# Matmul operands at multiples of 512 bytes, and 512-column products issued as two groups of 256 columns

## The reference

```python
# first block, one layer
h = h + _hybrid_mixer(_rmsnorm(h, ...), ..., w_in, ..., w_out)   # retention, gated delta, gated linear
h = h + _memory_cross_attn(_rmsnorm(h, ...), mem_n, wq, wk, wv, wo)
h = h + _conv_ffn(_rmsnorm(h, ...), ffn_up, ffn_conv_w, ffn_down)
# second block, two layers
for l in range(2):
    z = rms_norm(x, g_attn[l]) @ w_in[l]
    ...                                # MLA, dilated and top-k attention on slices of z
    x = x + mix @ w_o[l]
    u = causal_dwconv(rms_norm(x, g_ffn[l]) @ w_up[l], conv_w[l], conv_b[l])
    gate, up = u[..., :D_FF], u[..., D_FF:]
    x = x + (jax.nn.silu(gate) * up) @ w_down[l]      # D_FF = 2816
return rms_norm(x, g_final)
```

## The kernel before

| operand | slot 0 | slot 1 |
|---|---|---|
| `w_hi` | 384 | 0 |
| `w_lo` | 128 | 256 |
| `hT_hi`, `hT_lo` | 192 | 192 |
| `a_hi`, `a_lo` | 480 | 480 |

## Time and profile before

### The profile page before, as it was taken

The page is one execution under the profiler, slowest core; times in us unless marked ns, Lnnn a source line. Parts: engine busy times, 40 slices in busy tenths (PEclk is TensorE's granted clock), DMA queues, the critical chain, the costliest instruction groups (busy, mean ns, idle before and its releaser), DMA issues.

```text
span 1482.9 us, 20646 instructions
## 1 busy us (share of the span) xinstructions
PE 1306.5 (88%) x7800; PEld 1161.0 (78%) x7800; DVE 886.5 (60%) x1502; ACT 637.9 (43%) x1007; POOL 41.7 (3%) x51
## 2 busy tenths in 40 slices
PE   6993885679888899998898988999979899799996
PEld 6982664568778789997896667999979766699995
DVE  5436665542664676766656547676664664766674
ACT  4443101112544455554544345555544433555553
POOL 0000211000200000000000000000000000000000
PEclk9995766887999999999897589999999957899998
DMA  8430000001442455453430034454345101454541
GB/s 329 172 129 28 0 0 29 1 1 57 142 151 105 153 191 202 179 196 120 178 142 29 1 130 158 177 205 173 138 171 193 57 1 56 161 196 173 204 174 42
DMA packets 20228, 183.26 MB, mean 124 GB/s; under 512 B 2368, under 2 KB 2640, under 8 KB 4560
## 3 DMA queue, kind: packets, MB, share of 16 engines
q1 hardware_dynamic: 19040, 178.09, 33.2%
q0 software_dynamic: 1136, 4.46, 0.9%
HBM read 181.49 MB, written 1.05 MB: 123 GB/s over the span
## 4 chain that ended last, share of the span: by engine, by line
PE 80%; DVE 11%; ACT 5%; issue 1%; POOL 1%; DMA 1%; SPq 0%; DVEq 0%; ACTq 0%; POOLq 0%
PE ps L486 21%; PE ps L488 21%; PE ps L487 21%; PE ps L656 3%; PE ps L637 3%; PE ps L647 2%; PE ps L772 2%; PE ps L745 1%; ACT z L1026 1%; ACT hT_hi L1036 1%; DVE arena L1823 1%; ACT w_hi L1016 1%; DVE arena L1605 1%; DVE w_lo L1329 1%; PE ps L954 1%
## 5 line engine op out<-in xcount | busy, mean ns | idle before, releaser
L1329 DVE TENSOR_TENSOR w_lo<-raw,w_hi 128x2048 fp32r<-128x2048 f32 (+4 forms) x252 | 390.8, 1557 | 167.7 <-ACT w_hi L1016 167.1
L1016 ACT ACTIVATE w_hi<-raw 128x2048 fp32r<-128x2048 f32 (+4 forms) x252 | 332.2, 1325 | 215.4 <-PE ps L488 200.9
L486 PE MATMUL ps<-hT_hi,w_hi 128*128 128x256 f32 x1184 | 336.8, 284 | 8.2 <-DVE hT_lo L1378 8.2
L488 PE MATMUL ps<-hT_hi,w_lo 128*128 128x256 f32 x1184 | 335.0, 283 | 0.0
L487 PE MATMUL ps<-hT_lo,w_hi 128*128 128x256 f32 x1184 | 334.8, 283 | 0.0
L486 PEld LDWEIGHTS ps<-hT_hi,w_hi 128*128 128x128 f32 x1184 | 228.9, 193 | 13.7 <-issue 7.8
L487 PEld LDWEIGHTS ps<-hT_lo,w_hi 128*128 128x128 f32 x1184 | 228.4, 193 | 2.8
L488 PEld LDWEIGHTS ps<-hT_hi,w_lo 128*128 128x128 f32 x1184 | 228.6, 193 | 0.0
L486 PE MATMUL ps<-w_hi,hT_hi 128*128 128x378 f32 (+2 forms) x576 | 209.7, 364 | 18.2 <-DVE hT_lo L1463 9.6
L487 PE MATMUL ps<-w_lo,hT_hi 128*128 128x378 f32 (+2 forms) x576 | 207.8, 361 | 0.0
L488 PE MATMUL ps<-w_hi,hT_lo 128*128 128x378 f32 (+2 forms) x576 | 207.7, 361 | 0.0
(11 more groups left out here) (274 smaller groups left out, 1462.3 us busy)
## 6 DMA issues: line engine op xcount, KB each, us to landing
raw<-in_ffn_b SPq DMA_DIRECT2D x63, 1536.0 KB, 6.4
raw<-in_win SPq DMA_DIRECT2D x16, 1512.0 KB, 6.4
raw<-in_win SPq DMA_DIRECT2D x10, 1552.0 KB, 6.5
raw<-in_wo SPq DMA_DIRECT2D x12, 1024.0 KB, 4.8
raw<-in_wk SPq DMA_DIRECT2D x4, 1024.0 KB, 4.7
raw<-in_wv SPq DMA_DIRECT2D x4, 1024.0 KB, 4.8
raw<-in_wout SPq DMA_DIRECT2D x4, 1024.0 KB, 4.8
raw<-in_wq SPq DMA_DIRECT2D x4, 1024.0 KB, 4.7
```

The lines of the kernel that those rows point to most:

```text
L486: pe.matmul(out, a_hi_, b_hi, start=start, stop=False)
L488: return pe.matmul(out, a_lo_, b_hi, start=False, stop=stop)
L1016: act.activation(w_hi[:, slot, a:b], raw[:, slot, a:b], ACT.Copy).then_inc(hi_done, 1)
L1329: dve.tensor_tensor(w_lo[:, slot, a:b], raw[:, slot, a:b], w_hi[:, slot, a:b].bitcast(F32), ALU.subtract).then_inc(lo_done, 1)
```

## The change

1. The operands of the matmuls (`a_hi`, `a_lo`, `hT_hi`, `hT_lo`, `w_hi`, `w_lo`) and then `raw` are declared first, behind a filler `lead` of 96 elements, and a slot grows from 3104 to 3200 elements (12,800 bytes, 25 times 512). The scratch for POOL's transfers shrinks from 16,384 to 8,192 bytes, which makes the room. In the built program `a_hi` is now at 8,704, `a_lo` at 10,752, `hT_hi` at 12,800, `hT_lo` at 20,992, `w_hi` at 29,184, `w_lo` at 54,784: all of them, and both slots, at multiples of 512. The moving weights of the column stages still start at many remainders, since their rows stay 1,552 and 1,512 bytes long.
2. In the row stages a new helper `mm3_halves` makes two groups of three matmuls over 256 columns each out of every group of three over 512. `start` is set for the first half alone and `stop` for the second alone.

```diff
-SLOT = 3104
+SLOT = 3200
+LEAD = 96
...
-        raw = sb("raw", [P, 2, SLOT])
+        sb("lead", [P, LEAD])
+        a_hi = sb("a_hi", [P, 2, T], F32R)
+        a_lo = sb("a_lo", [P, 2, T], F32R)
+        hT_hi = sb("hT_hi", [P, KT, T], F32R)
+        hT_lo = sb("hT_lo", [P, KT, T], F32R)
         w_hi = sb("w_hi", [P, 2, SLOT], F32R)
         w_lo = sb("w_lo", [P, 2, SLOT], F32R)
+        raw = sb("raw", [P, 2, SLOT])
...
-        hT_hi = sb("hT_hi", [P, KT, T], F32R)
-        hT_lo = sb("hT_lo", [P, KT, T], F32R)
...
-        a_hi = sb("a_hi", [P, 2, T], F32R)
-        a_lo = sb("a_lo", [P, 2, T], F32R)
...
+            def mm3_halves(bank, a_hi_, a_lo_, b_hi, b_lo, start, stop):
+
+                for c in (slice(0, 256), slice(256, 512)):
+                    ins = mm3(bank[:, c], a_hi_, a_lo_, b_hi[:, c], b_lo[:, c], start and c.start == 0, stop and c.start > 0)
+                return ins
...
-                                ins = mm3(ps[:, 2 * t + half, :], hT_hi[:, k, t * P:(t + 1) * P],
+                                ins = mm3_halves(ps[:, 2 * t + half, :], hT_hi[:, k, t * P:(t + 1) * P],
...
-                            ins = mm3(ps[:, 2 * t + half, :], a_hi[:, a, t * P:(t + 1) * P],
+                            ins = mm3_halves(ps[:, 2 * t + half, :], a_hi[:, a, t * P:(t + 1) * P],
...
-                        ins = mm3(ps[:, 2 * t + half, :], a_hi[:, 1, t * P:(t + 1) * P], a_lo[:, 1, t * P:(t + 1) * P],
+                        ins = mm3_halves(ps[:, 2 * t + half, :], a_hi[:, 1, t * P:(t + 1) * P], a_lo[:, 1, t * P:(t + 1) * P],
...
-    nc = bacc.Bacc("TRN2", target_bir_lowering=False, num_devices=1)
+    nc = bacc.Bacc("TRN2", target_bir_lowering=False, num_devices=1, dynamic_dma_scratch_size=8192)
```

## The result

The changed kernel takes 1498.84 us in the median of 4 runs (1497.09 to 1499.74), the kernel before 1481.84 us in the median of 4 runs beside them. The ratio is 1.016 (95% interval 1.009 to 1.023). On another chip, with 6 and 17 runs, it was 1.011 (1.009 to 1.014). So the change costs 1.1 to 1.6%, 17 us between the medians, where I had forecast 33 to 37 us less.

What follows compares the result with a forecast made beforehand. TensorE's mm3 matmul pace was taken as the bound; (19.2 + 10.8 + 5.1 + 2.6) x 0.96 = 36.2 us off the profiled span 1482.9 gave 1446.7, forecast as a 1449 us median, 2.5% faster, range 1430 to 1474.

Steps and rivals of the forecast that it cites:

- What bounds the kernel: Feed-forward: TensorE is busy throughout, so the pace of mm3's matmuls decides the time and only a shorter pace shortens it.
- The reading of the two slots: up and stage V: slots differ only in address, and both operands' sides matter, by about 4 ns a matmul.
- I take 113.5 - 3.3 = 110.2 ns: Aligned 256-column matmuls: slot 1's pace less stage V's moving-operand effect, assuming the two effects add.
- my upper bound of 113.5: Aligned 256-column matmuls: slot 1's pace in ns, if the moving operand's 192 costs nothing; lower bound 109.4.
- Transposed stages: 3,552 matmuls going from 115.6 to 110.2 ns, 19.2 us less.
- Row stages: Split 512-column products at 220.4 ns a pair: down 10.8 us less, square stages 5.1 us less.
- Column stages: Stationary side aligned, moving side mixed: 2.1 ns less for each of 1,248 matmuls, 2.6 us.
- Share at the full clock: Whole kernel: about 3% of matmuls run at the lower clock, so the summed gain is multiplied by 0.96.
- no effect of addresses: Rival: slots differ by something accompanying them, such as DVE and ACT work; 1484 or 1489 us, chance 0.09.
- partial: Rival: effects do not add, 113.5 ns is the fp32r floor at 256 columns; 1471 us, within 2%, chance 0.28.
- My slower rival: Row stages: the second load of the same operand is exposed, a pair takes 380 ns; 1643 us, chance 0.03.
- if they still differ, the address was not it: Check in up: both slots should take about 5.29 us for 48; slots still differing would rule out the address.

Runs made afterwards that it cites:

- the faster layouts: Changed kernel with whole 512-column products, hT at 192, w at 0 (mod 256), a_hi and a_lo at 192 or 160: ratios 0.988 and 0.991 (192), 0.988 (160).
- `a` at 480: Changed kernel with whole 512-column products, hT at 192, w at 0, a_hi and a_lo at 480 (224 mod 256): 1481.73 us, ratio 0.999.
- Kernels of TensorE alone: Whole computation left out, only runs of fp32r matmuls with weight loads at varied operand starts and orders; 256 columns at difference 0 took 120.0 ns.
- one layout: Changed kernel with whole 512-column products, hT at 192, w at 0, a_hi and a_lo at 160 (mod 256): 1467.99 us, ratio 0.988.
- the feed-forward that stayed at 117.8 behind difference 192: Changed kernel, whole 512-column products, hT and a at 192, w at 0 (mod 256), one feed-forward per profile at 8.42 us rounds: ratio 0.988, again 0.991.
- hT at 64: Changed kernel with whole 512-column products, hT_hi and hT_lo at 64, w and a at 0 (mod 256): 1483.67 us, ratio 1.003.

## Why the prediction was wrong

- *What bounds the kernel*: right. The pace of `mm3`'s matmuls decided, no wait ahead of them grew by more than 0.1 us, and the smaller scratch cost nothing that shows (it is in all the faster layouts too, though no run changes it alone).
- *The reading of the two slots*: the step that failed. I took "the stationary operand goes to 0 and 256, 4.2 ns less" and "in stage V the moving operand makes that step, 3.3 ns less" for two effects, one of each operand's own remainder. The runs show a pace that goes with the difference of the two starts instead: it went from 192 to 64 in `up` and from 64 to 192 in stage V. The paces fitted either reading, since in each stage only one operand had moved. The sign gives it away in hindsight: difference 64 is the faster for 256 columns and the slower for 512. And the 4.2 ns lay between the two paces of difference 64, not between two addresses: at slot 1's addresses `up` also takes 117.7, as slot 0 does, in every other of slot 1's rounds with only the split, and in nearly all rounds with `a` at 480.
- *"I take 113.5 - 3.3 = 110.2 ns"*: measured 120.0. It was an extrapolation to a pair of addresses that no row showed, and my upper bound of 113.5 was no bound: nothing I had excluded a pair worse than all those seen. Transposed stages: +15.6 us (3,552 x 4.4 ns) instead of -19.2.
- *Row stages*: 240 ns a pair instead of 220.4, the same step carried over. Down +4.8 us instead of -10.8; square +4.3 instead of -5.1. Here the split matters: at difference 0 whole matmuls of 512 columns would have gained (229 and 227 ns), and the split traded that for two of the slowest kind. At the addresses before, the split by itself cost little: ratio 1.005 (1.000 to 1.009), by the paces 3 us in `up` and 1 in down.
- *Column stages*: 177.1 to 176.7 ns, and 173.3 to 173.1, -0.3 us instead of -2.6. Their moving rows start at many remainders, before and after.
- *Share at the full clock*: the terms add up to 24.4 us, times 0.96 = 23.4, and the span grew by 14.5, the median by 17. The rest lies in the stretches at the lower granted clock, where 256 columns take 213 ns at any address. They fell differently in these two executions. Over 333 to 371 us, stage K in both, the clock was 0.77 before and is 0.89 now:

```profile
333.00:371.00 38.00, 36.46 (x258) 32.91 (x258) 11.56 (x19) 7.81 (x9) 0.00 (x0) 0.89 0.20 71
```

  There the changed kernel did 258 matmuls, the kernel before 229, and stage K took 37.2 us from its first to its last matmul instead of 41.9. I had said the lower clock would not move since those stages were left as they are; it did, and stage K is one of the transposed stages that the change touches. This stretch is an example and not the whole account: in the changed kernel's second profile its clock was 0.82 and the span the same, 1497.0. Over all executions, an estimate at equal mean clock by the line in the last section puts the change at 23 to 24 us, what the terms give.
- *Rivals*: "no effect of addresses" is refuted, "partial" too. My slower rival had the right sign and the wrong cause: the loads are not exposed by their length; the pace goes with where the load and the moving operand start. I gave it 3%, because I had looked for harm only in the split and took alignment for something that can at worst do nothing.
- *What would show it wrong*: "if they still differ, the address was not it". They no longer differed, and the pace was one that I had not listed. Nothing in the list asked whether slot 1's pace would last at the same addresses, on which the upper bound of 113.5 stood.

## What to carry to other kernels

The start of an operand has no good value by itself here. For fp32r products that reload their weights each time, look at the difference between the start of the next stationary and the current moving operand, and never set both on the same large multiple without measuring. Two buffers of one double-buffered stage that run at different paces are a free experiment on addresses; before extrapolating from it, write down every quantity that differs between the two, differences of addresses included. A pace read in one slot can hang on what its neighbour leaves behind, so it is no bound for another layout. Kernels of TensorE alone gave a map that foretold one layout's paces to 0.6 ns. It did not foretell the feed-forward that stayed at 117.8 behind difference 192, nor slot 1 of the kernel before. The layout measured 1.2% faster, of which its paces explain about half.

## What was not expected of the hardware

- Matmuls of 256 columns in fp32r with a load each take from 113.3 to 120.2 ns at the full clock, and those of 512 from 226.7 to about 235, by the difference of two addresses mod 256 bytes and by what ran ahead. The best of 256 columns doubled, 226.6, is the best of 512, so a split gains nothing over a whole matmul at its best. At difference 64 it can: with only the split, chunk 2 of stage V took 5.45 us for 24 pairs, 227.1 ns each, and the whole matmuls 232.5 before.
- TensorE's pace has memory. At difference 64 two steady paces, 113.3 and 117.7 ns, hold for 20 rounds, and what ran ahead picks one. Other differences have two paces as well: 256 columns at 96, 128, 192 and 224, and 512 columns at 192 (228.9 and 233.3). At difference 0, 256 columns stood at 120 in every run. What carries the memory is not shown.
- The Trainium skill, page "TensorE: Matmul & The Clock Gate", section "Step-by-step: what each phase is for", gives TensorE two independent read ports and says that loading the next weights does not steal read bandwidth from the running matmul. For 128 columns (111.5 ns at all addresses) and for 256 at the lower clock (213 ns in all layouts) these runs show nothing against it. At 256 and 512 columns at the full clock they speak against it, if the dependence on the two starts is such a contention. That it is one was argued from the period and the difference, not shown.
- The kernel before spreads over 1463 to 1488 us. The changed kernel and the one with hT at 64, whose transposed matmuls have one pace, spread over 4 and 3 us. But the one with only the addresses, with one pace too, spreads over 21. The spread goes with the granted clock: three of its ten executions took 1473 to 1474 us at a mean clock of 0.90, the others 1489 to 1493 at 0.883 to 0.887. Over the 73 executions of the kernel before that ran beside the experiments, time falls by 11.5 us for each 0.01 of mean clock (correlation -0.89). What moves the clock from one execution to the next stays open.
